# Hybrid encoder trunk: post-norm and residual moved into the feed-forward's last group, preparation parameters loaded in z projection

## The reference, cut to what matters

```python
def rms_norm(x, g, eps=EPS):
    xf = x.astype(jnp.float32)
    y = xf * lax.rsqrt(jnp.mean(xf * xf, -1, keepdims=True) + eps)
    return (y * g.astype(jnp.float32)).astype(x.dtype)

        x = x + rms_norm(mix, p['norm_mix_post'][layer])
        h = rms_norm(x, p['norm_ffn_pre'][layer])
        f = jnp.square(jax.nn.relu(h @ p['w_ff1'][layer])) @ p['w_ff2'][layer]
        x = x + rms_norm(f, p['norm_ffn_post'][layer])
```

## Time and profile before

| what | before |
|---|---|
| median of three runs | 4616.34 us |
| the profiled execution's own time | 4612.09 us |
| its span (first to last instruction) | 4610.3 us |
| mean granted TensorE clock | 0.938 of 2.4 GHz |
| PE busy | 4185.4 us (91%), 24128 matmuls |
| DVE, ACT, POOL busy | 2202.1, 1394.4, 1154.7 us |
| scaling by the post gain, L238 | 30 instructions of 1281 ns |
| old rows' addition, L230 | 30 instructions, 2352 to 2364 ns (medians) |
| spreading of the gains, L275 | 96 matmuls of 418 ns, overlapping |

### The profile page before, as it was taken

The page is one execution under the profiler, slowest core; times in us unless marked ns, Lnnn a source line. Parts: engine busy times, 40 slices in busy tenths (PEclk is TensorE's granted clock), DMA queues, the critical chain, the costliest instruction groups (busy, mean ns, idle before and its releaser), DMA issues. The chain is left out here.

```text
span 4610.3 us, 62817 instructions
## 1 busy us (share of the span) xinstructions
PE 4185.4 (91%) x24128; PEld 3628.4 (79%) x24128; DVE 2202.1 (48%) x3169; ACT 1394.4 (30%) x2256; POOL 1154.7 (25%) x647
## 2 busy tenths in 40 slices
PE   7999696999989999769999999879997899999997
PEld 6889565888888888658888888767886788888885
DVE  5643244555555555654443333456663343333334
ACT  4321363333333333242111111234553321111111
POOL 1120134333333333131111111113331311111112
PEclk8999777999999999879999999879999999999998
DMA  4221583111111110231111111120002211111112
GB/s 124 73 92 63 156 302 120 47 53 47 49 47 47 47 47 19 89 130 46 36 36 36 43 39 36 51 71 9 7 1 83 82 42 36 37 45 36 36 36 91
DMA packets 205270, 287.08 MB, mean 62 GB/s; under 512 B 31185, under 2 KB 148241, under 8 KB 205089
## 3 DMA queue, kind: packets, MB, share of 16 engines
q1 hardware_dynamic: 205088, 284.45, 18.6%
HBM read 206.42 MB, written 77.99 MB: 62 GB/s over the span
## 5 line engine op out<-in xcount | busy, mean ns | idle before, releaser
L691 DVE TENSOR_TENSOR top_acc<-top_acc,ffn_down 128x512 f32<-128x512 f32 x600 | 412.6, 688 | 374.8 <-PE ffn_down L110 374.8
L108 PE MATMUL ffn_bank<-hT_ffn_high,ffn_w_high 128*128 128x512 f32 (+1 forms) x1536 | 544.9, 355 | 4.9 <-DVE hT_ffn_low L662 4.9
L110 PE MATMUL ffn_bank<-hT_ffn_high,ffn_w_low 128*128 128x512 f32 (+1 forms) x1536 | 544.3, 354 | 0.0
L109 PE MATMUL ffn_bank<-hT_ffn_low,ffn_w_high 128*128 128x512 f32 (+1 forms) x1536 | 544.2, 354 | 0.0
L108 PE MATMUL ffn_down<-ffn_w_high,ffn_f_high 128*128 128x512 f32 x1280 | 498.3, 389 | 0.0
L109 PE MATMUL ffn_down<-ffn_w_low,ffn_f_high 128*128 128x512 f32 x1280 | 498.3, 389 | 0.0
L110 PE MATMUL ffn_down<-ffn_w_high,ffn_f_low 128*128 128x512 f32 x1280 | 497.9, 389 | 0.0
L680 DVE TENSOR_TENSOR ffn_square<-ffn_relu 128x512 f32<-128x512 f32 (+1 forms) x192 | 146.6, 764 | 641.1 <-ACT ffn_relu L625 641.1
L649 POOL TENSOR_TENSOR ffn_w_low<-up_w_raw,ffn_w_high 128x2048 fp32r<-128x2048 f32 x32 | 147.6, 4611 | 737.8 <-ACT ffn_w_high L631 722.7
L108 PEld LDWEIGHTS ffn_bank<-hT_ffn_high,ffn_w_high 128*128 128x128 f32 x1536 | 290.9, 189 | 46.7 <-issue 5.7
L109 PEld LDWEIGHTS ffn_bank<-hT_ffn_low,ffn_w_high 128*128 128x128 f32 x1536 | 291.0, 189 | 41.0
(11 more groups left out here) (430 smaller groups left out, 9040.8 us busy)
## 6 DMA issues: line engine op xcount, KB each, us to landing
up_w_raw<-in_w_ff SPq DMA_DIRECT2D x64, 1024.0 KB, 5.3
project_w_raw<-in_w_in_even SPq DMA_DIRECT2D x27, 512.0 KB, 5.1
s_tm_both<-prepare_tb SPq DMA_DIRECT2D x20, 512.0 KB, 7.3
s_fm_dir<-prepare_fd SPq DMA_DIRECT2D x20, 512.0 KB, 6.5
scan_tb<-s_tm_both SPq DMA_DIRECT2D x20, 512.0 KB, 3.5
scan_fb<-s_fm_both SPq DMA_DIRECT2D x20, 512.0 KB, 4.2
scan_fd<-s_fm_dir SPq DMA_DIRECT2D x20, 512.0 KB, 4.8
norm_x_old<-s_x SPq DMA_DIRECT2D x20, 512.0 KB, 4.6
```

Source lines behind the costliest of these rows:

```text
L108: pe.matmul(out, stationary[0], moving[0], start=start, stop=False)
L109: pe.matmul(out, stationary[0], moving[1], start=False, stop=False)
L110: return pe.matmul(out, stationary[1], moving[0], start=False, stop=stop)
L691: dve.tensor_tensor(a, a, out_of(u), ALU.add).then_inc(added, 1)
```

## The change

1. `acc` is allocated at the start of the program. norm0's rows and, in project, `padded`, `mixed` and two of the three raw weight buffers lie in it (class `FirstTokens`), and so do prepare's parameters and its first tile's `rk` and `qkv`. All of them are loaded by project's SP stream after the last shifted block's taps and ahead of the z stores. prepare's SP stream begins with `load_rk(1)`.
2. In `feed_forward` the last group is written out beside the loop on PE and DVE. After tile 0 of its down product PE spreads the gain. ACT squares each tile when both halves are added; DVE scales tile t - 1 after the additions of tile t; POOL adds old rows that SP has loaded into the weights' raw buffers (four rows' room); SP stores, and the phase ends when the stores have landed.
3. norm2 keeps only the pre-norm and transposition, on `acc` as it lies, with no loads and no stores. norm4 is gone: ffn1 stores to the outputs.

```diff
+class FirstTokens:
+    def __init__(self, E, room):
+        flat = room[:, :, :].rearrange("p t d -> p (t d)")
...
+        self.padded = [rows(j * PADDED, PADDED) for j in range(3)]
+        at = 3 * PADDED
+        self.mixed = [rows(at + j * SPAN, SPAN) for j in range(3)]
+        at += 3 * SPAN
+        self.w_raw = [rows(at + j * KB * P, KB, P) for j in range(2)]
...
@@ in_projections, sync
+            sp.wait_ge(taps_done, 3 * TURNS + CREDIT)
+            sp.dma_start(after.a_log, ins["gdn_A_log"]...).then_inc(after.rate_params, 16)
+            sp.dma_start(after.dt, ins["gdn_dt_bias"]...).then_inc(after.rate_params, 16)
+            for d in range(2):
+                sp.dma_start(after.incl[d], ins["c_incl"][d]).then_inc(after.rate_params, 16)
+                sp.dma_start(after.excl[d], ins["c_excl"][d]).then_inc(after.rate_params, 16)
+                sp.dma_start(after.a0[d], vector(ins["rwkv_a0"][0][d]), allow_slow_non_contiguous=True)...
...
+            for j in range(3):
+                sp.wait_ge(stored[j], 32 * (TURNS + 1))
+            sp.dma_start(after.norm_rows, ins["c_norm_rows"]).then_inc(after.params, 16)
+            sp.dma_start(after.rk, shift_dst.rearrange("b p n -> p b n")[:, :, 0:P]).then_inc(after.rk_loaded, 16)
+            sp.dma_start(after.qkv, conv_dst.rearrange("b p n -> p b n")[:, :, 0:P]).then_inc(after.qkv_loaded, 16)
             for t in range(TILES):
                 sp.wait_ge(z_done, t + 1)
                 sp.dma_start(z_dst[t], z[t % 2][:, :]).then_inc(z_stored[t % 2], 16)
...
@@ feed_forward
+    gain = ups[0]
+    x_old = [raw[:, :, :].rearrange("p a b -> p (a b)")[:, h * D:(h + 1) * D] for raw in (w1_raw, w2_raw) for h in range(2)]
...
+            sp.wait_ge(w1_low, GROUPS)
+            load(0)
+            load(1)
+            sp.wait_ge(w2_low, GROUPS)
+            load(2)
+            load(3)
+            for t in range(TILES):
+                sp.wait_ge(x_updated, t + 1)
+                if t + RING < TILES:
+                    load(t + RING)
+                sp.dma_start(of(x_dst, t), acc[:, t, :]).then_inc(x_stored, 16)
+            sp.wait_ge(x_stored, 16 * TILES)
...
+            def spread():
+                pe.wait_ge(relu_done, UP * GROUPS + 4)
+                n_rows = gain_rows.shape[0]
+                for k in range(KB):
+                    row = ident[0:n_rows, g_post + k:g_post + k + 1].broadcast_to([n_rows, P])
+                    last = pe.matmul(gain[:, k // 4, (k % 4) * P:(k % 4 + 1) * P], row, gain_rows[:, :], start=True, stop=True)
+                last.then_inc(gain_done, 1)
...
                 for t in range(TILES):
+                    if last_group and t == 1:
+                        spread()
...
-            with pe.Fori(0, GROUPS - 1) as i:
+            with pe.Fori(0, GROUPS - 2) as i:
                 group(i + 1, False)
+            group(LAST, False, True)
...
+            for t in range(TILES):
+                act.wait_ge(added, DOWN * LAST + (2 * t + 2 + 4))
+                act.activation(squares[:, :], acc[:, t, :], ACT.Square, accum_out=col(sq, t)).then_inc(mix_squares, 1)
+                act.wait_ge(mix_squares, t + 1)
+                act.activation(col(rt, t), col(sq, t), ACT.Sqrt, bias=eps[:, :], scale=1.0 / D).then_inc(mix_root, 1)
...
+            for t in range(TILES):
+                pool.wait_ge(x_loaded[t % RING], 16 * (t // RING) + 16)
+                pool.wait_ge(mix_scaled, t + 1)
+                pool.tensor_tensor(acc[:, t, :], acc[:, t, :], x_old[t % RING], ALU.add).then_inc(x_updated, 1)
...
+            def scale(t):
+                dve.wait_ge(mix_root, t + 1)
+                dve.reciprocal(col(rc, t), col(rt, t)).then_inc(mix_inverse, 1)
+                dve.wait_ge(mix_inverse, t + 1)
+                if t == 0:
+                    dve.wait_ge(gain_done, 1)
+                dve.scalar_tensor_tensor(two(acc[:, t, :]), two(acc[:, t, :]), col(rc, t), gain[:, :, :],
+                                         ALU.mult, ALU.mult).then_inc(mix_scaled, 1)
...
+                    if last_group and u % 2 == 1 and u >= 3:
+                        scale(u // 2 - 1)
...
+            group(LAST, False, True)
+            scale(TILES - 1)
...
@@ program
-                phase("norm2", residual_norm, x_mid, x_mid, hT, ident, gain_rows, acc, gain("norm_ffn_post", 0), gain("norm_mix_pre", 1))
+                phase("norm2", residual_norm, None, None, hT, ident, gain_rows, acc, None, gain("norm_mix_pre", 1))
...
-            phase("ffn1", feed_forward, acc, ident, hT, acc, up)
-        phase("norm4", residual_norm, x_mid, x_out, None, ident, gain_rows, acc, gain("norm_ffn_post", 1), None)
+            phase("ffn1", feed_forward, acc, ident, hT, acc, up, gain_rows, gain("norm_ffn_post", 1), x_mid, x_out)
```

More of the change, by code:

```diff
@@ L190, in _ @@
                 for t in range(1, TILES):
-                    if t >= AHEAD:
+                    if t >= AHEAD and x_src is not None:
                         sp.wait_ge(loaded[t % AHEAD], 16 * (t // AHEAD))
@@ L204, in x_root_of @@
                     act.wait_ge(x_updated, t + 1)
-                else:
+                elif x_src is not None:
                     act.wait_ge(loaded[t % AHEAD], 16 * (t // AHEAD) + 16)
@@ L284, in _, with rows, in_projections @@
                     last.then_inc(turned, 1)
-def in_projections(nc, E, hT, w_in, gates, conv_w, mu, o_norm_w, conv_dst, shift_dst, z_dst):
+class FirstTokens:
+    def __init__(self, E, room):
+        flat = room[:, :, :].rearrange("p t d -> p (t d)")
+        def rows(at, *shape, n=P):
+            size = math.prod(shape)
+            ap = flat[0:n, at:at + size]
+            return ap.rearrange("p (a b) -> p a b", a=shape[0]) if len(shape) == 2 else ap
+        self.padded = [rows(j * PADDED, PADDED) for j in range(3)]
[3 more added lines that the diff above has]
+        self.w_raw = [rows(at + j * KB * P, KB, P) for j in range(2)]
+        assert at + 2 * KB * P <= TILES * D
+        self.w2, self.a2, self.g2 = (rows(j * RW, RW) for j in range(3))
+        self.w0 = rows(3 * RW, 2 * RW)
+        self.ones = rows(5 * RW, P)
+        self.incl = [rows(5 * RW + (1 + d) * P, P) for d in range(2)]
+        self.excl = [rows(5 * RW + (3 + d) * P, P) for d in range(2)]
+        self.norm_cols = rows(5 * RW + 5 * P, 3 * GH, NORMS)
+        small = 5 * RW + 5 * P + 3 * GH * NORMS
+        self.head_cols = rows(small, 2)
+        self.a_log, self.dt = (rows(small + 2 + j * 2 * GH, 2 * GH) for j in range(2))
+        small += 2 + 4 * GH
+        self.a0 = [rows(small + d * RB, RB) for d in range(2)]
+        self.k_k, self.k_a, self.r_k = (rows(small + (2 + j) * RB, RB) for j in range(3))
+        assert small + 5 * RB <= 3 * PADDED
+        at = 3 * PADDED
+        self.norm_rows = rows(at, 3 * GH, P, n=NORMS)
+        self.rk = rows(at + 3 * GH * P, RWKV_BLOCKS, P)
+        self.qkv = rows(at + (3 * GH + RWKV_BLOCKS) * P, CONV_BLOCKS, P)
+        self.params, self.rate_params = E.sem("params"), E.sem("rate_params")
+        self.rk_loaded, self.qkv_loaded = E.sem("rk_loaded"), E.sem("qkv_loaded")
+def in_projections(nc, E, hT, w_in, gates, conv_w, mu, o_norm_w, conv_dst, shift_dst, z_dst, ins, after):
     CONV, SHIFT = CONV_BLOCKS // 3, RWKV_BLOCKS // 3
@@ L370, in _ @@
                 sp.dma_start(z_dst[t], z[t % 2][:, :]).then_inc(z_stored[t % 2], 16)
-            for j in range(3):
-                sp.wait_ge(stored[j], 32 * (TURNS + 1))
             for j in range(2):
@@ L517, in __init__, with feed_forward @@
         self.w1_loaded, self.w2_loaded = E.sem("w1_loaded"), E.sem("w2_loaded")
-def feed_forward(nc, E, rows, ident, hT, acc, up):
+def feed_forward(nc, E, rows, ident, hT, acc, up, gain_rows, g_post, x_src, x_dst):
     GB = 2
@@ L549, in part, with of, col, two @@
         return slice(None), slice(None), slice(t * P, (t + 1) * P)
+    def of(views, t):
+        return views[0][:, t, :] if t < TILES_P else views[1][:, t - TILES_P, :]
+    def col(v, t):
+        return v[:, t:t + 1]
+    def two(ap):
+        return ap.rearrange("p (a n) -> p a n", a=2)
     with nc.Block() as block:
@@ L697, in _, with prepare_tokens @@
             group(0, True)
-            with dve.Fori(0, GROUPS - 1) as i:
+            with dve.Fori(0, GROUPS - 2) as i:
                 group(i + 1, False)
-def prepare_tokens(nc, E, ins, ident, eps, gates, rates, conv_fm, shift_fm, fm_both, fm_dir, tm_both, tm_dir):
+            group(LAST, False, True)
+            scale(TILES - 1)
+            dve.wait_ge(mix_scaled, TILES)
+def prepare_tokens(nc, E, ins, ident, eps, gates, rates, conv_fm, shift_fm, fm_both, fm_dir, tm_both, tm_dir, first):
     def two(name, shape):
         return [E.sb(f"{name}_{j}", shape) for j in range(2)]
-    qkv = two("qkv", [P, CONV_BLOCKS, P])
-    rk = two("rk", [P, RWKV_BLOCKS, P])
+    qkv = [first.qkv, E.sb("qkv_1", [P, CONV_BLOCKS, P])]
+    rk = [first.rk, E.sb("rk_1", [P, RWKV_BLOCKS, P])]
```

(6 more changed lines are left out.)

103 lines of the change are left out of this document (56 added, 47 removed).

## The result

The changed kernel takes 4571.24 us (median of 4 runs, 4565.24 to 4575.54), the one before 4616.28 (4 runs beside it, 4612.2 to 4619.13): ratio 0.9902, 95% interval 0.9885 to 0.9919. The forecast was 4568, range 4557 to 4583. The profiled execution took 4570.8 us (span 4569.0, mean granted clock 0.943); the forecast for it was 4563.8. The work has not changed: PE is busy for 4185.0 us now, 4185.4 before.

The account below looks back on a forecast made before the run. PE was taken to bound the matmul stages, leaving gains where it stands still between phases. 20.2 + 3.9 + 24.2 = 48.3 us off 4612.1 gave 4563.8 profiled, plus 4.25 for the median: 4568, range 4557 to 4583.

Parts of the forecast that it names:

- Prepare's start: Start of prepare: with parameters and tile 0 loaded early, DVE's chain starts right behind its memset; gain 20.2 us.
- the two terms: Start of prepare: chain begins 19.8 us earlier, and POOL starting its products behind DVE saves another 0.4 us.
- the upper end: Start of prepare: 21.6 us gained if POOL's second four products begin only after the rates are done.
- z projection: z stores behind SP's prefetch issues: first store landed by 462.4 at the latest, 2.1 us before PE's need; cost 0.
- Spreading and the down product: Last group of each feed-forward: gain spreading costs 2.0 us, DVE, ACT and POOL beside the down product cost 0.
- ffn0 and norm2: ffn0's last addition to norm2's ACT start 11.5 us, norm2 35.9 instead of 50.67; net gain 3.9 us.
- ffn1 and the end: After ffn1's last addition: 10.8 us to the end instead of 37.0, plus 2.0 for spreading; gain 24.2 us.
- the first (z stalls): z projection: late z store 0 makes PE's tile 6 begin 6.9 us late; time 4575, chance 0.06.
- The second (prepare bound by something else): Prepare: second tile's loads or a first-tile wait give back 8 of the 20 us; time 4576, chance 0.05.
- The third: Last groups: DVE late at 3.0 us a tile against 2.72, costing 2.5 us twice; time 4573, chance 0.06.
- fifth: norm2: the pre-norm alone is as long as before, bound by ACT and transposes, costing 14.8; time 4583, chance 0.03.
- The fourth: Last groups: DVE and POOL exclude each other, 4.95 us or more a tile; time 4613 to 4624, chance 0.04.

Follow-up runs that it names:

- e8: Changed kernel with POOL's first four products of tile 0 held back until DVE has made the last rate copy; 4570.38 us (one run).
- e6: The changed kernel timed again, unaltered, in a later sitting; 4568.12 us, ratio 0.9901 to the kernel before.
- e4: Changed kernel with rk and qkv of tile 0 loaded two more times, each pair waited for, ahead of the first z store; 4587.4 us (one run).
- e3: Kernel before with only ffn0's post-norm moved and norm2 shortened, ffn1 and norm4 as before; 4611.07 us, ratio 0.9995.
- e2: Kernel before with only the post-norms moved into both feed-forwards, norm2 shortened, norm4 gone, old preparation; 4592.1 us, ratio 0.9955.
- the two parts alone: Kernel before with only the preparation's part, 4594.01 us; kernel before with only the new feed-forwards and norms, 4592.1 us.
- e9: Changed kernel with eight throw-away PE products ahead of each next tile's load wait in prepare's loop, two other waits moved ahead; 4538.65 us, ratio 0.9840.
- e10: The filling products of e9 put into the three-edit kernel e5; 4526.46 us, ratio 0.9808 to the kernel before.
- e7: Changed kernel with DVE instead of POOL adding the last tile's old rows in both feed-forwards; 4573.4 us (one run).
- e5: Changed kernel with POOL's tile 0 products after the rates, DVE adding the last old rows, ffn0's stores waited for in norm2; 4561.69 us, ratio 0.9891.

## Why the prediction was right, point by point

- **Prepare's start.** Forecast 20.2; from the phase's start (495.04 before, 497.25 after) to PE's first matmul it fell from 28.2 to 8.06 us: 20.1. Inside it the two terms were off and made up for each other: the chain began 20.05 us earlier (forecast 19.8), and POOL's start beside it gave 0.1 us (8.00 to 7.90 from L1034's place to PE) and not 0.4. L1037 was read as the one step held up by POOL; five are, before and after. For the upper end only POOL's second set was to move; e8 moved both sets and gained 2.75 us, against the 1.4 between forecast and upper end. In PE's idle time the gain is 19.7 us in this profile and 20.5 in e6.
- **z projection.** Forecast cost 0, store landed by 462.4; it was 461.7. That these agree is partly luck: the store left at 454.6 and not 452.4 and took 7.1 us and not 10; all but one of the small loads' issues took 0.35 to 0.51 us, the biases' two not 2.2 each, but qkv's own took 5.59. The margin was put at 2.1 us and is 4.9 by e4: that PE's tile 6 needs tile 2 read out is right, ACT only comes to it sooner.
- **Spreading and the down product.** Forecast 2.0 and 0 a feed-forward; the last groups are 2.20 us longer, of which 2.05 is the spreading and 0.15 the rest. DVE's tile was put at 2.6 us against PE's 2.72. It took 2.72, since an addition is 0.67 here and not the 0.6 read from two start times. The cover is used up: DVE has next to no idle time left in these tiles, and what is added to it there would make it fall behind PE tile by tile. No run tried it.
- **ffn0 and norm2.** Forecast 11.5 and 35.9, measured 11.20 and 35.91, gain 4.0 with the 2.20 off (forecast 3.9). e3 agrees: this half is worth next to nothing in time.
- **ffn1 and the end.** Forecast 10.8 after the last addition, gain 24.2; measured 11.01 and 23.8.
- **The sum** of these is 47.9 against 48.3. The profiled execution gained 41.3 and not 48.3 because of stages that were booked at nothing: project began its z matmuls 2.0 us later (430.9 to 432.8), the tile loop took 3.2 more, scan 2.5 more. e6, the same kernel, had 155.97 and 1147.95 in these two and e2, with the old preparation, 166.63: they vary by themselves, and the forecast's mistake was to compare one profile of each kernel without a term for that. The medians gained 45.0 us here and 43.8 beside e6, and the two parts alone 18.8 and 20.7. So 3 to 4 us of the 48.3 stay open: with one profile of the kernel before, it is not shown that none of it is a price of the change. Its z matmuls begin earlier than in all thirteen others (by 0.8 to 3.3 us, e2 and e3 with the old projection among them), and its tile loop is the shortest but for e9 and e10.

Of the rivals, the first (z stalls) was shown to be real 4.9 us away (e4). The second (prepare bound by something else) has its place, the waits for qkv, but they were there before. The third and fifth are out by the windows and by norm2's 35.91. The fourth, mutual exclusion on DVE and POOL in the last group, did not happen: the additions and scalings there have one tensor in SBUF and one in PSUM, and keep 0.68 to 0.69 and 1.28 us beside POOL. With both operands in SBUF it is real, as in e7. By the Trainium skill (SBUF — State Buffer, Who interferes with whom) a VectorE instruction that needs its second port and a GpSimd one exclude each other; e7's addition agrees (issued 0.75 us before POOL's end, it ends 1.08 us after it), and so do the steps of the rates, L1149 and the copies with one SBUF tensor among them: the same section counts tensor_scalar and copy among the operations that can take both ports, and in e8 they are short. The Trainium skill's order of descriptors on one issuing engine (DMA: Bandwidth & Descriptors, HWDGE ordering) agrees with the z store: issued at 454.6, it landed 7.1 us later behind rk and qkv, where a 512 KB store alone takes 2.6.

## What to carry to other kernels

Moving a phase's steps under the last group of a bound engine pays where nothing follows (23.8 us at the end) and hardly where a phase follows (4.0 at norm2), since the tail to the last landed store is then bare; price each place by itself. Prefetched parameters pay in full only as long as what is queued behind them has its margin, so measure the margin by making them late once. And before believing a few microseconds of a small edit in a looped kernel, look for idle time put down to issue at one line of a loop and for instruction packets in the DMA queues: 72 throw-away products were worth 23 to 28 us of scan here, about as much as either half of the change.

## What the runs showed that was not expected

- A loop's instructions can be loaded anew each turn: 9 packets and 2.3 to 3.7 us of PE standing per turn of scan, with PE at 1.2 GHz (0.51) for 7 us after the one looked at. 72 small products ahead, in either of two places, end it; 36 do not. The best version has them in the tile loop's waits, where that stage took no longer, with the three edits of e5: 4526.46 us, ratio 0.9808 where the changed kernel has 0.9902.
- Behind a DMA wait of 3.11 us the tile loop's 24 products took 5.48 us instead of 2.94, yet holding the clock up did not pay there: at 0.85 instead of 0.75 the loop still took 154.6 us.
- A DMA issue can hold its queue for 5.59 us (qkv behind rk and 19 small loads), where the small ones take 0.43.
- Beside POOL's 1.04 us products, DVE steps of 0.20 to 0.24 us take 0.96 to 1.10, whether they read one SBUF tensor or two; it cost the start of prepare 2.75 us.
